# Attention layer of a hybrid encoder: the values of two head pairs by block products, woven between query and key tiles

## The reference, cut to what matters

```python
qkv = x @ w_qkv                                  # 2048 x 6144: queries, keys, values
q = q.reshape(B, S, H, 2, d) * (d ** -0.5)       # H = 8 heads, d = 128, two maps per head
k = k.reshape(B, S, H, 2, d)
v = v.reshape(B, S, H, 2 * d)
...
    s = jnp.einsum('bqhjd,bkhjd->bhjqk', q_blk, k)
    s = jnp.where(allowed, s, -jnp.inf)
    p = jax.nn.softmax(s, axis=-1)
    w = p[:, :, 0] - lam_full * p[:, :, 1]
    return jnp.einsum('bhqk,bkhe->bqhe', w, v)
...
o = rms_norm(o, subln) * (1.0 - lam_init)
y = o @ w_o
h = layer_norm(DN_ALPHA * h + y, ln_g, ln_b)
```

## Time and profile before

| what | value |
|---|---|
| runs (us) | 2103.27, 2102.74, 2103.27; median 2103.27 |
| the profiled execution: span from first to last instruction | 2101.5 us |
| what lies around the span, against the runs | 1.2 to 1.8 us |
| PE busy | 2096.6 us, 100% |
| DVE / ACT / POOL busy | 84% / 57% / 9% |
| granted TensorE clock | 1.000 |
| HBM traffic | 231 GB/s over the span |

### The profile page before, as it was taken

The page is one execution under the profiler, slowest core; times in us unless marked ns, Lnnn a source line. Parts: engine busy times, 40 slices in busy tenths (PEclk is TensorE's granted clock), DMA queues, the critical chain, the costliest instruction groups (busy, mean ns, idle before and its releaser), DMA issues.

```text
span 2101.5 us, 27096 instructions
## 1 busy us (share of the span) xinstructions
PE 2096.6 (100%) x10924; PEld 1803.2 (86%) x10924; DVE 1762.8 (84%) x1504; ACT 1202.8 (57%) x1083; POOL 191.8 (9%) x156
## 2 busy tenths in 40 slices
PE   9999999999999999999999999999999999999999
PEld 8888888988888888888898888889888888888887
DVE  6555659978988989989788888797989989989888
ACT  5454545456656656666465565544655666666563
POOL 3000000300000000000030022102000000000000
PEclk9999999999999999999999999999999999999999
DMA  9445456579889888888845778766789889888884
GB/s 325 166 142 198 163 177 212 195 228 287 240 230 290 244 254 263 252 240 239 301 141 189 217 225 242 278 216 220 211 250 262 261 235 262 248 274 245 230 247 179
DMA packets 241905, 487.37 MB, mean 232 GB/s; under 512 B 7872, under 2 KB 8128, under 8 KB 240768
## 3 DMA queue, kind: packets, MB, share of 16 engines
q1 hardware_dynamic: 204928, 406.48, 54.4%
q0 software_dynamic: 36288, 78.39, 20.5%
q10 hardware_dynamic: 576, 0.92, 0.1%
HBM read 483.66 MB, written 2.10 MB: 231 GB/s over the span
## 4 chain that ended last, share of the span: by engine, by line
PE 100%; DVE 0%; issue 0%; DVEq 0%; POOL 0%; POOLq 0%
PE ps L696 59%; PE ps L1045 9%; PE ps L1043 9%; PE ps L1049 8%; PE ps L923 2%; PE ps L980 1%; PE ps L985 1%; PE ps L978 1%; PE ps L1261 1%; PE ps L1255 1%; PE ps L1257 1%; PE ps L1277 1%; PE ps L1275 1%; PE ps L1282 1%; PE ps L1296 1%; PE ps L771 1%
## 5 line engine op out<-in xcount | busy, mean ns | idle before, releaser
L696 PE MATMUL ps<-X,hi 128*128 128x512 f32 (+1 forms) x3008 | 697.1, 377 | 0.1
L696 PEld LDWEIGHTS ps<-X,hi 128*128 128x128 f32 x3008 | 549.4, 188 | 99.5 <-DVE X L1911 0.3
L1593 ACT ACTIVATE hi<-raw 128x2048 fp32r<-128x2048 f32 x196 | 372.6, 1915 | 233.5 <-DVE raw L2321 151.1
L2307 DVE TENSOR_TENSOR lo<-raw,hi 128x2048 fp32r<-128x2048 f32 x196 | 445.0, 2288 | 19.6 <-PE ps L1049 10.4
L696 PE MATMUL ps<-X,lo 128*128 128x256 f32 x2816 | 387.0, 283 | 0.0
L696 PEld LDWEIGHTS ps<-X,lo 128*128 128x128 f32 x2816 | 373.3, 191 | 12.7
L1885 DVE TENSOR_TENSOR lo<-raw,hi 128x2048 fp32r<-128x2048 f32 x104 | 237.6, 2297 | 97.4 <-ACT hi L1364 92.5
L1364 ACT ACTIVATE hi<-raw 128x2048 fp32r<-128x2048 f32 x118 | 224.3, 1913 | 151.5 <-PE ps L696 111.0
L2307 DVE TENSOR_TENSOR lo<-up_raw,hi 128x2048 fp32r<-128x2048 f32 x112 | 256.3, 2288 | 32.3 <-PE ps L696 32.3
L1577 ACT ACTIVATE hi<-up_raw 128x2048 fp32r<-128x2048 f32 x112 | 214.3, 1913 | 24.3 <-PE ps L1049 11.2
L1045 PE MATMUL ps<-hi,forms 128*128 128x512 f32 x448 | 175.7, 392 | 0.0
(11 more groups left out here) (298 smaller groups left out, 2853.8 us busy)
## 6 DMA issues: line engine op xcount, KB each, us to landing
raw<-in_mlp_w_dram SPq DMA_DIRECT2D x144, 1024.0 KB, 7.7
up_raw<-in_mlp_w_dram SPq DMA_DIRECT2D x112, 1024.0 KB, 7.7
raw<-in_mlp_w_dram POOLq DMA_DIRECT2D x56, 1024.0 KB, 9.5
raw<-in_gla_w_in_dram SPq DMA_DIRECT2D x48, 1024.0 KB, 5.6
raw<-in_attn_w_qkv_dram SPq DMA_DIRECT2D x47, 1024.0 KB, 5.2
raw<-in_attn_w_o_dram SPq DMA_DIRECT2D x16, 1024.0 KB, 5.5
raw<-in_gla_w_o_dram SPq DMA_DIRECT2D x16, 1024.0 KB, 6.5
raw<-in_gla_w_in_dram POOLq DMA_DIRECT2D x8, 1024.0 KB, 9.0
```

The costliest lines, as they stand in the source:

```text
L696: return pe.matmul(o, w, m, start=start, stop=stop)
L1593: act.activation(hi[:, P_AT[p] % 4], raw[:, slot], ACT.Copy).then_inc(hi_ready, 2 if p == PRODUCTS - 1 else 1)
L2307: dve.tensor_tensor(lo[:, at % 3], src, hi[:, at % 4].bitcast(F32), ALU.subtract).then_inc(lo_ready, n)
```

## The change

The values of head pairs 1 and 2 are no longer two values groups of 96 matmuls. They are made in two **units** of seven block products: unit u takes rows 1024u to 1024u + 1023 of the weights and the 1024 value columns of both pairs. Unit 0 is woven with the four query tiles of pair 1, unit 1 with its key tiles. Seven products of 12 matmuls in each unit make 168 matmuls in place of 192. The order of groups is then: queries 0, keys 0, values 0, unit 0 (counted as groups 3 to 5), unit 1 (groups 6 to 8), queries 2 (9), keys 2 (10), queries 3 (11), keys 3 (12), values 3 (13), output projection from 14.

The results of the units are gathered in `v_unit_rows`: four kept by ACT (`keep_v`) and nine additions on DVE (`v_add`, counter `v_added`). The forms and these rows stand in `res`, so the x of the residual is loaded again (2 MB) when pair 2 is weighed, and scaled on POOL then; POOL's four small loads so come at the very start. Scores of pairs 1 and 2 are now made in the queries group of the next pair and weighed in its keys group, in other banks than before. All loops over pairs are written out.

The core of the diff, PE first:

```diff
-            with pe.Fori(0, PAIRS - 1) as c:
-                v_group(3 * c + 2, c)
-                pe.wait_ge(v_copied, 2 * c + 1)
-                pe.wait_ge(maxes, 8 * c + 8)
-                pe.wait_ge(mixedT_ready, 2 * c + 1)
-                cols_group(3 * c + 3, 0, X, {
...
-                pe.wait_ge(v_copied, 2 * c + 2)
-                pe.wait_ge(o_lo, 2 * c + 2)
-                cols_group(3 * c + 4, 1, X)
+            def v_unit(u):
...
+                if u == 0:
+                    pe.wait_ge(v_copied, 1)
+                    pe.wait_ge(maxes, 8)
+                    pe.wait_ge(mixedT_ready, 1)
+                else:
+                    pe.wait_ge(halves_added, 6)
+                up_tile(g, 0)
+                if u == 0:
+                    weigh_values(0, 0, 0)
+                    turn_mixed(1, 1)
...
+                fg_product(g, 0, BANK, plain(0, 0), True)
+                if u == 0:
+                    weigh_values(1, 1, 0)
+                up_tile(g, 1)
...
+                fg_product(g, 1, BANK + 1, form(S1), True)
+                if u == 0:
+                    turn_output(0, 0)
+                    turn_output(1, 1)
+                up_tile(g, 2)
...
+            def scores_of(c):
+                return {(0, 1): lambda: scores(2 * c, 0, c), (1, 0): lambda: scores(2 * c + 1, 1, c),
+                        (2, 0): lambda: turn_mixed(2 * c, 0), (3, 0): lambda: turn_mixed(2 * c + 1, 1)}
+
+            def outputs_of(c):
+                return {(0, 1): lambda: (weigh_values(2 * c, 0, c), weigh_values(2 * c + 1, 1, c)),
+                        (2, 0): lambda: (turn_output(2 * c, 0), turn_output(2 * c + 1, 1))}
+
+            v_group(G_V[0], 0)
+            v_unit(0)
+            v_unit(1)
+            pe.wait_ge(halves_added, 8)
+            pe.wait_ge(v_added, 9)
+            cols_group(G_Q[2], 0, X, scores_of(1))
+            pe.wait_ge(maxes, 16)
+            pe.wait_ge(mixedT_ready, 4)
+            pe.wait_ge(halves_added, 10)
+            cols_group(G_K[2], 1, X, outputs_of(1))
+            pe.wait_ge(o_lo, 4)
+            pe.wait_ge(halves_added, 12)
+            cols_group(G_Q[3], 0, X, scores_of(2))
+            pe.wait_ge(maxes, 24)
+            pe.wait_ge(mixedT_ready, 6)
+            pe.wait_ge(halves_added, 14)
+            cols_group(G_K[3], 1, X, outputs_of(2))
+            pe.wait_ge(o_lo, 6)
```

DVE's order around unit 0 and at the end of unit 1 (`unit_lo` and `unit_up_lo` make a `lo` tile, `unit_sum` a sum of two weight tiles):

```diff
+            softmax_max(0, 0)
+            v_form_whole(1)
+            mix_maps(0, 0)
+            unit_up_lo(0, 0)
+            softmax_max(1, 1)
+            v_form_sums(1)
+            mix_maps(1, 1)
+            unit_lo(0, 0)
+            unit_sum(0, 1)
+            v_form_low(1)
+            unit_up_lo(0, 1)
+            unit_lo(0, 1)
+            unit_sum(0, 2)
+            normalise(0, 0)
+            unit_up_lo(0, 2)
+            normalise(1, 1)
...
+            add_halves(3, 0, kT)
+            dve.wait_ge(v_added, 4)
+            v_add(1, 4, 1, 0, ALU.subtract)
+            unit_lo(1, 6)
+            qk_low(3, kT, k_hi, k_lo)
+            late_lo(G_Q[2], 0, -2)
+            dve.wait_ge(v_added, 5)
+            v_add(1, 5, 2, 1)
+            late_lo(G_Q[2], 1, 0)
+            dve.wait_ge(v_kept, 4)
+            v_add(1, 6, 3, 0)
+            split_lo(G_Q[2], 2)
...
+            def lo_of(g, at, src, n=1):
+                dve.wait_ge(hi_ready, 4 * g + at + 1)
+                dve.wait_ge(w_used, 4 * g + at - 2)
...
+            def late_lo(g, j, free):
+                dve.wait_ge(w_used, 4 * g + free)
+                split_lo(g, j)
```

ACT's order at the start of unit 0 (`unit_hi` and `unit_up_hi` make a `hi` tile; `unit_hi(0, 1)` waits for `unit_sum(0, 1)`), and POOL's list at the start:

```diff
+            exps(0, 0)
+            copy_v(0, (first_block_done, 1), v_rows[:, 0, :])
+            unit_up_hi(0, 0)
+            exps(1, 1)
+            copy_mixedT(0, 0)
+            v_form_high(1)
+            unit_hi(0, 0)
+            copy_v(1, (w_used, 4 * G_V[0] + 4), v_rows[:, 1, :])
+            unit_up_hi(0, 1)
+            unit_hi(0, 1)
+            copy_mixedT(1, 1)
...
-            scale_residual(0)
             pool.dma_start(lam_rows.rearrange("p a b -> p (a b)"),
...
+            third_sum(0)
+            rms_power(0, 0)
+            rms_power(1, 1)
+            fourth_sum(0)
+            third_sum(1)
+            fourth_sum(1)
+            for c in range(1, PAIRS):
+                if c == PAIRS - 1:
+                    pool.wait_ge(x_back, 16 * TB)
+                    scale_residual(0)
```

More of the change, by code:

```diff
@@ L89 @@
 RES_MLP = [RES_OUT, RES_GWO + RES_OUT]
-ROWS_WO = PAIRS
+ROWS_WO = 2
+V_COPIES = 4
 ROWS_MLP = [ROWS_WO + 2, 0]
@@ L751, in cols_group @@
                                j == 0 and k == 0, False)
+                    if after and (j, 0) in after:
+                        after[j, 0]()
                     pe.wait_ge(lo_ready, 4 * g + j + 1)
@@ new lines, in fg_product @@
+            def fg_product(g, p, bank, stationary, start):
+                at = P_AT[p]
+                acc = ps[:, bank, :]
+                pe.wait_ge(hi_ready, 4 * g + at + 1)
+                for k in range(KPT):
+                    a_hi, a_lo = stationary(k)
+                    pe.matmul(acc, a_hi, hi[:, at % 4, k, :], start=start and k == 0, stop=not start,
+                              skip_group_check=not start)
+                    pe.matmul(acc, a_lo, hi[:, at % 4, k, :], start=False, stop=not start, skip_group_check=not start)
+                pe.wait_ge(lo_ready, 4 * g + at + 1)
+                for k in range(KPT):
+                    a_hi, a_lo = stationary(k)
+                    m = pe.matmul(acc, a_hi, lo[:, at % 3, k, :], start=False, stop=k == KPT - 1 or not start,
+                                  skip_group_check=not start)
+                m.then_inc(w_used, 2 if p == PRODUCTS - 1 else 1)
@@ L1019, in _ @@
             last_out_group(G_WO + 4, 2, 2, F, 1)
[L1022 to L1051, removed]
             def fused(m, i, c, at_start=False):
@@ new lines, in _ @@
+            unit_hi(0, 6)
+            qk_high(2, qT, q_hi)
+            unit_up_hi(1, 0)
+            unit_hi(1, 0)
+            keep_v(3, 6, BANK)
+            unit_up_hi(1, 1)
+            unit_hi(1, 1)
+            unit_up_hi(1, 2)
+            unit_hi(1, 2)
+            unit_hi(1, 3)
+            unit_up_hi(1, 3)
+            unit_hi(1, 4)
+            unit_hi(1, 5)
+            copy_halves(G_UNIT[1], 3, 0, qk_half, 1, 1.0, U_AT[3] + 1)
+            unit_hi(1, 6)
+            qk_high(3, kT, k_hi)
@@ new lines, in v_add, with v_form_whole @@
+            def v_add(u, p, at, bank, op=ALU.add):
+                dve.wait_ge(w_used, 4 * G_UNIT[u] + P_AT[p] + 1)
+                r = v_unit_rows[:, at, :]
+                dve.tensor_tensor(r, r, ps[:, BANK + bank, :], op).then_inc(v_added, 1)
+            def v_form_whole(u):
+                a, b = slice(8 * u, 8 * u + KPT), slice(8 * u + KPT, 8 * u + 2 * KPT)
+                for f, k, t in ((S3, a, 1), (S1, b, 1), (S2, a, 0), (S4, b, 0)):
+                    dve.tensor_tensor(v_whole[u][:, f, :, 1, :], X[:, k, 0, blk(t)].bitcast(F32),
+                                      X[:, k, 1, blk(t)].bitcast(F32), ALU.add).then_inc(v_whole_ready, 1)
@@ new lines, in _ @@
+            unit_sum(0, 2)
+            normalise(0, 0)
+            unit_up_lo(0, 2)
+            normalise(1, 1)
+            unit_lo(0, 2)
+            unit_lo(0, 3)
+            o_lo_head(0, 0)
+            o_lo_head(1, 1)
+            unit_up_lo(0, 3)
+            unit_lo(0, 4)
+            unit_lo(0, 5)
+            add_halves(2, 0, qT, Q_SCALE)
+            dve.wait_ge(v_kept, 2)
+            v_add(0, 4, 1, 0, ALU.subtract)
+            unit_lo(0, 6)
+            qk_low(2, qT, q_hi, q_lo)
@@ new lines, in _ @@
+            unit_up_lo(1, 0)
+            dve.wait_ge(v_kept, 3)
+            v_add(0, 5, 2, 1)
+            unit_lo(1, 0)
+            unit_sum(1, 1)
+            unit_up_lo(1, 1)
+            unit_lo(1, 1)
+            unit_sum(1, 2)
+            v_add(1, 0, 0, 0)
+            unit_up_lo(1, 2)
+            dve.wait_ge(v_added, 1)
+            v_add(1, 1, 1, 1)
+            unit_lo(1, 2)
+            unit_lo(1, 3)
+            unit_up_lo(1, 3)
+            dve.wait_ge(v_added, 2)
+            v_add(1, 2, 2, 0, ALU.subtract)
@@ new lines, in _ @@
+            unit_lo(1, 4)
+            dve.wait_ge(v_added, 3)
+            v_add(1, 3, 0, 3)
+            unit_lo(1, 5)
+            add_halves(3, 0, kT)
[9 more added lines that the diff above has]
+            v_add(1, 6, 3, 0)
@@ new lines, in _ @@
+            split_lo(G_Q[2], 2)
+            for c in (1, 2):
+                q, k = G_Q[c + 1], G_K[c + 1]
+                softmax_max(2 * c, 0)
+                split_lo(q, 3)
+                mix_maps(2 * c, 0)
+                softmax_max(2 * c + 1, 1)
+                split_lo(k, 0)
+                mix_maps(2 * c + 1, 1)
+                split_lo(k, 1)
+                split_lo(k, 2)
+                add_halves(2 * c + 2, 0, qT, Q_SCALE)
+                qk_low(2 * c + 2, qT, q_hi, q_lo)
+                split_lo(k, 3)
```

(1 more changed line is left out.)

384 lines of the change are left out of this document (290 added, 94 removed).

## The result

The changed kernel takes 2124.68 us (median of 4 runs, 2123.78 to 2127.21) against 2103.08 before: a ratio of 1.0104 (95% interval 1.0092 to 1.0116), so 21.6 us slower. The forecast was 2116.4 with a range up to 2124.0: right in sign and in its main mechanism, too small in size, and the median lies 0.7 us above the range. The profiled execution has a span of 2122.4 us, 20.9 more than before.

The account below looks back on a forecast made before the run. PE, busy throughout, was taken as the bound: -5.7 saved, +8.7 group boundaries, +5.0 before group 9, +4.1 unit 0, +1.0 start give +13.1 us, so 2116.4 us, range 2109.5 to 2124.

Parts of the forecast that it names:

- Saved, 5.7 us: Values of pairs 1 and 2: two groups of 96 matmuls, 43.8 us, become fourteen products, 38.1 us; 5.7 us saved.
- Group boundaries, 8.7: Before groups 10, 11 and 12 PE waits for additions of the group just finished: 3 x 2.9 = 8.7 us lost.
- Before group 9, 5.0: PE waits for the ninth addition, DVE's chain of 13.1 us against three products of 8.2: 5.0 us lost.
- Unit 0, 0.5 + 1.0 + 2.6: PE waits in unit 0 on both mixed-map copies (0.5, 1.0) and the second normalisation (2.6): 4.1 us lost, 1.5 to 8.
- The start, 1.0: POOL's small loads, coming some 23 us earlier, slow the first transfers: 1.0 us lost, between 0 and 2.4.
- The sign named for this term: If the first tile still starts at 7.9 us, the loss at the start is nothing.
- The clock, 0: Rival, 13%: PE's clock falls behind the new gaps, giving 2119 to 2122, four full falls 2139; nothing in the sum.
- +18.7 us: Alternative estimate by the skill's idle-gap rule: the sum +13.1 with one tile's stretch at the lower clock.
- Everything is covered: Rival, 5%: ACT and DVE keep pace, no boundary waits, the saved matmuls stand: 2097.6 us.
- The units starve: Rival, 12%: `lo` tiles or accumulating loads come late in products 4 to 6: +5, 2121 us.
- The covers named for the forms, the accumulating loads, the reload of x and POOL's queue: This added work was claimed hidden under other work, without PE waits; the nearest accumulating load has 4 us to spare.
- The range: Forecast 2109.5 to 2124 us; the upper end takes in starving units and one fall of the clock, not several.

Follow-up runs that it names:

- Experiment 8: Changed kernel with boundary and ninth-addition waits behind the next group's first tile, small loads held back, unit 0's second weight sum behind the second normalisation: 2100.59 us.
- Experiments 1 and 6: 1: changed kernel, three boundary waits moved behind next group's first tile, 2111.81 us; 6: kernel before, one wait added ahead of each keys group, 2117.45 us.
- experiment 7: Kernel before with POOL's four small loads issued ahead of its scaling of the residual, nothing else: 2105.43 us.
- Experiment 4: Changed kernel with small throw-away matmuls keeping PE at work in the four gaps at group boundaries: 2119.24 us.
- experiment 3: Changed kernel with POOL's four small loads held until all eight quarters of x are turned: 2123.87 us.
- experiment 5: Changed kernel with DVE's second sum of weights in unit 0 moved behind the two normalisations: 2123.22 us.

## Why the prediction was off, point by point

- **Saved, 5.7 us.** Right by its mechanism. The units' window, 82.79 to 172.90, is 90.11 us against the forecast "near 90"; that it agrees so well is partly luck, since 0.7 us less of waits meets 0.8 more of work. What the woven order adds, some 1.5 us in all, was taken at nothing, so the net is 4.2. Experiment 8 gives the same: its span is 2.5 us shorter than before, with 2.2 us of waits left in unit 0 and keys 0 begun 0.5 earlier.
- **Group boundaries, 8.7.** Measured 2.97 + 2.81 + 2.97 = 8.75. Experiments 1 and 6 show both ways round that it is the placed wait.
- **Before group 9, 5.0.** Measured 4.89. The chain holds as well: from the end of the last key tile at 164.54 to the end of the ninth addition at 177.68 it is 13.1 us, as forecast, and PE's three products take 8.4.
- **Unit 0, 0.5 + 1.0 + 2.6.** Measured 0.44, 0.57 and 2.31, so 3.3 for 4.1, each in its place.
- **The start, 1.0.** This term was mis-sized: 2.0 (2.2 by experiment 7). I took about the middle of the range 0 to 2.4 with the argument that only the first tile has no slack. The 345 and 318 GB/s show that the loads while they ran cost nearly their whole upper bound, and the wait of 1.31 us for x at 12.65 us shows that the next quarter had no slack either. The sign named for this term was a wrong one too: the first tile starts at 7.86 us, against 7.91 before, so it read "nothing" where 2.0 us were lost behind it.
- **The clock, 0.** This is the step that failed. The text named it, priced it (2.7 us for a product, 5.6 for a tile) and gave 13% to it as a rival, on the ground that no row had PE idle for longer than 1.1 us. But the forecast itself made four such gaps, so the clock belonged in the sum. Experiment 4 shows the cause, and it is 6.1 of the 20.9 us in the profile: three falls, of 2.8, 1.7 and 1.7 us. The lower of the two prices fits the dearest of them; none cost a full tile's 5.6. With it and the start the sum would have been 13.1 + 6.1 + 1.0 = 20.2, or 2123.5. The Trainium skill ("TensorE: Matmul & The Clock Gate", section "Why this matters for your kernels") warns against idle gaps between bursts of matmuls because the array then goes back to the lower clock; the windows at 0.55 and 0.68 agree, and that rule, quoted ahead of the run with +18.7 us, was nearer than the rows alone.
- **The rivals.** "Everything is covered" fell with the waits list. "The units starve" fell too: in unit 1 and in products 4 to 6 of unit 0 PE does not wait. The covers named for the forms, the accumulating loads, the reload of x and POOL's queue held: no wait of PE on any of them stands in the list.
- **The range.** It held one fall of the clock on top of a late end elsewhere; three falls and the dearer start together went past it.

## What to carry to other kernels

Before a wait is put ahead of a group, ask what its releaser waits for: if that is the last tile of the group just finished, the wait costs the whole chain between the engines, every time, and it should stand where the bank is first written. Price a new gap on a busy PE twice, by its length and by the first tile behind it at the lower clock, and put both in the sum. Where a fix shows less than it should in the total, look in the trace whether the rest came back somewhere else: experiment 3 was hidden by clock falls until its timeline was read.

## What the runs showed of the hardware

- In the profiles of these runs the clock fell behind all 4 gaps of 4.9 us (tile of 5.34 to 6.63 us), behind 12 of 15 gaps of 2.8 to 3.0 us (5.33 to 6.61), and behind 3 of 5 gaps of 2.3 us in which PE had nothing to do. The same gap in the same code did so in one kernel and not in another that differs elsewhere: the 2.3 us one in unit 0 not in the changed kernel, but with the small loads later. What decides it no run shows. I had not expected it behind the short ones. A fall cost mostly 1.7 us, at times 2.8.
- The time of the changed kernel scatters by 3.4 us over four runs; with spins in the long gaps it is 0.2, with the gaps gone 0.8 over eleven. That the gaps cause the scatter is not shown: experiment 5 keeps the four long ones and scatters by 0.8, and experiment 7 has none and scatters by 2.1 over ten runs.
- Four loads of 0.53 MB together, issued between 2.2 and 5.5 us, lowered what the busy DMA engines moved from 390 and 387 to 345 and 318 GB/s in the windows from 5 to 15 us, and the kernel took 2.0 to 2.2 us longer. Which of the four does it, and why, was not tested.
